# Two chunk loops with the 64x64 inverse issued as ten single products, one other block between each two

## The reference, cut to what matters

```python
def gdn_core(q, k, v, g, beta, s0):
    ...
    kb = k * beta[..., None]
    a_kk = jnp.einsum('bnhid,bnhjd->bnhij', kb, k) * jnp.exp(jnp.where(strict, seg, -jnp.inf))
    rhs = jnp.concatenate([kb * jnp.exp(gcum)[..., None], v * beta[..., None]], axis=-1)
    sol = lax.linalg.triangular_solve(a_kk, rhs, left_side=True, lower=True, unit_diagonal=True)
    ...
    a_qk = jnp.einsum('bnhid,bnhjd->bnhij', q, k) * jnp.exp(jnp.where(incl, seg, -jnp.inf))
    ...
    def step(s, xs):
        w_n, u_n, aqk_n, q_n, k_n, gl_n = xs
        v_new = u_n - w_n @ s
        o_n = q_n @ s + aqk_n @ v_new
        s = s * gl_n[..., None, None] + jnp.swapaxes(k_n, -1, -2) @ v_new
        return s, o_n

def rwkv_core(r, w, k, v, z, b, s0):
    def step(s, xs):
        r_t, w_t, k_t, v_t, z_t, b_t = xs
        sz = jnp.einsum('bhvk,bhk->bhv', s, z_t)
        s = (s * w_t[:, :, None, :] + sz[..., None] * b_t[:, :, None, :]
             + v_t[..., None] * k_t[:, :, None, :])
        return s, jnp.einsum('bhvk,bhk->bhv', s, r_t)
```

## Time and profile before

| | us |
|---|---|
| median of 3 runs | 2844.28 (2839.02 to 2854.64) |
| profiled execution | 2840.01 |
| its span, first to last instruction | 2838.3 |
| TensorE busy | 2509.7 (88%) |
| VectorE busy | 1565.3 (55%) |
| GpSimd busy | 837.4 (30%) |
| DeltaNet's chunk loop | 730.8 to 988.65 |
| the wide loop | 1165.7 to 1438.7 |

### The profile page before, as it was taken

The page is one execution under the profiler, slowest core; times in us unless marked ns, Lnnn a source line. Parts: engine busy times, 40 slices in busy tenths (PEclk is TensorE's granted clock), DMA queues, the critical chain, the costliest instruction groups (busy, mean ns, idle before and its releaser), DMA issues. The chain is left out here.

```text
span 2838.3 us, 72517 instructions
## 1 busy us (share of the span) xinstructions
PE 2509.7 (88%) x27195; PEld 1379.0 (49%) x27196; DVE 1565.3 (55%) x2859; ACT 968.9 (34%) x1707; POOL 837.4 (30%) x654
## 2 busy tenths in 40 slices
PE   5999899799677679789969897899999999999956
PEld 2448358445577645588844352333333333333322
DVE  3106276735367722556544486566666666666638
ACT  2603116312212112322211112455555555555511
POOL 1000000000343100111100002666666666666555
PEclk9999999899899989999979998999999999999978
DMA  6001302210000020000032207899998889772277
GB/s 254 2 0 46 137 15 90 87 36 1 2 3 4 3 72 1 2 4 4 4 113 89 101 1 294 303 344 350 366 354 315 336 323 352 271 296 89 74 298 317
DMA packets 109101, 408.12 MB, mean 144 GB/s; under 512 B 21002, under 2 KB 37084, under 8 KB 83933
## 3 DMA queue, kind: packets, MB, share of 16 engines
q1 hardware_dynamic: 76636, 287.71, 27.5%
q0 software_dynamic: 20736, 75.51, 6.8%
q10 hardware_dynamic: 11520, 41.95, 3.7%
HBM read 346.40 MB, written 58.72 MB: 143 GB/s over the span
## 5 line engine op out<-in xcount | busy, mean ns | idle before, releaser
L3198 PE MATMUL bank<-arena 128*32 x1280 | 567.4, 596 | 10.8 <-SPq L68 6.9
L3200 PE MATMUL bank<-arena 128*32 128x512 f32 x3840 | 568.4, 596 | 0.0
L3159 POOL COPY arena<-arena 128x2048 f32 x240 | 450.2, 1909 | 329.5 <-PE bank L3232 311.6
L3198 PEld LDWEIGHTS bank<-arena 128*32 128x32 f32 x1280 | 134.7, 110 | 358.6 <-issue 349.7
L3229 PE MATMUL bank<-arena 128*32 x640 | 289.3, 595 | 5.5 <-POOL arena L3159 5.5
L3232 PE MATMUL bank<-arena 128*32 128x512 f32 x1920 | 290.4, 595 | 0.0
L3353 DVE COPY arena<-arena 128x2048 f32 x80 | 138.5, 1731 | 203.8 <-PE bank L3200 185.8
L3290 ACT COPY arena<-arena 128x2048 f32 x80 | 152.0, 1900 | 204.4 <-PE bank L3200 142.9
L1255 PE MATMUL bank<-arena 64*64 64x64 f32 x4480 | 164.9, 224 | 58.3 <-DVE arena L1325 27.4
L3149 POOL DMA_INDIRECT arena<-normed_rows,arena x80 | 165.0, 2063 | 149.4 <-DVE arena L3337 137.4
L1255 PEld LDWEIGHTS bank<-arena 64*64 64x64 f32 x4480 | 149.1, 138 | 68.5 <-ACT arena L1315 22.0
(11 more groups left out here) (555 smaller groups left out, 4555.8 us busy)
## 6 DMA issues: line engine op xcount, KB each, us to landing
arena<-in_exp_w_gate_dram SPq DMA_DIRECT2D x64, 1024.0 KB
arena<-in_exp_w_up_dram SPq DMA_DIRECT2D x64, 1024.0 KB
arena<-in_exp_w_down_dram SPq DMA_DIRECT2D x64, 1024.0 KB
expert_rows<-arena ACTq DMA_DIRECT2D x80, 512.0 KB
arena<-in_w_mod_dram SPq DMA_DIRECT2D x32, 512.0 KB, 8.4
arena<-in_x_dram SPq DMA_DIRECT2D x16, 512.0 KB, 8.3
arena<-in_w_mod_dram SPq DMA_DIRECT2D x8, 1024.0 KB, 17.8
arena<-in_w_in_dram SPq DMA_DIRECT2D x12, 384.0 KB
```

The lines of the kernel that those rows point to most:

```text
L3159: last = nc.gpsimd.tensor_copy(down_copy(u), down_of(slots[u]))
L3198: nc.tensor.matmul(out(SUB - 1), XTT[:, b.q, c, rows(SUB - 1)], W[:, :, c], start=first, stop=end)
L3200: last = nc.tensor.matmul(out(u), XTT[:, b.q, c, rows(u)], WC[:, u, :, c], start=first, stop=end)
```

## The change: ten separate products, and grams, operands and turns split to lie between them

`weave` takes a table of stages with shifts (0: this pair, 1: the one ahead, -1: behind, 2: two ahead) and serves both loops; `weave_wide` is gone. The inverse's products are named, each is a stage of its own, and `fourth` and `eighth` stand apart from `y2` and `y4`. In DeltaNet the key gram is split into `rows` and `grams`, the query gram into `query rows` and `query grams`, and VectorE's part of the scan into `against` and `decay`. In the wide loop the four grams, the two operand groups (keys, queries) and the two turned operands (k, b) are stages of their own with semaphores of their own. The turn of the next pair's N0 moves from the head of its iteration to before t64 or y64 of the one before. No arithmetic is added or taken away; GpSimd's list in DeltaNet has its two stages under new names.

```diff
-    def tensor(self, pe, k, p):
+    def tensor(self, pe, what, p):
         N0, N32, N64, Y = (b[:, p % 2] for b in (self.N0, self.N32, self.N64, self.Y))
-        if k == 1:
-            self.dve_done(pe, p, "turned")
+        if what == "square":
+            pe.wait_ge(self.turned, p + 1)
             for n in range(2):
                 self.squared(n, self.M, N0)
-        elif k == 2:
+        elif what == "y2":
             self.act_done(pe, p, "square1")
-            self.dve_done(pe, p, "y1")
+            pe.wait_ge(self.begun, p + 1)
+            if p >= 1:
+                self.dve_done(pe, p - 1, "y64")
             self.product(2, self.N, Y)
+        elif what == "fourth":
             for n in range(2):
                 self.dve_done(pe, p, f"square{n}_turned")
                 self.squared(n, self.M, self.N)
-        elif k == 3:
+        elif what == "y4":
             self.act_done(pe, p, "fourth1")
             self.dve_done(pe, p, "y2")
             self.product(2, self.N, Y)
+        elif what == "eighth":
             for n in range(2):
                 self.dve_done(pe, p, f"fourth{n}_turned")
                 self.squared(n, self.M, self.N)
-        elif k == 4:
...
+        if what == "turn":
+            turn(self.M, self.N0[:, p % 2]).then_inc(self.turned, 1)
+            dve.wait_ge(self.turned, p + 1)
+            self.nc.vector.tensor_tensor(Y, self.M, each(self.c.ident, 8), ALU.add).then_inc(self.begun, 1)
+        elif what in ("square", "fourth"):
+            if what == "square":
+                dve.wait_ge(self.begun, p + 1)
             for n in range(2):
-                self.act_done(dve, p, f"square{n}")
-                turn(self.M[:, 4 * n:4 * n + 4], self.N[:, 4 * n:4 * n + 4])
-        elif k == 2:
-            add("y2", "y1")
-            for n in range(2):
-                self.act_done(dve, p, f"fourth{n}")
-                turn(self.M[:, 4 * n:4 * n + 4], self.N[:, 4 * n:4 * n + 4])
-        elif k == 3:
-            add("y4", "y2")
-        elif k == 4:
-            add("y8", "y4")
-        elif k == 5:
+                self.act_done(dve, p, f"{what}{n}")
+                turn(self.M[:, 4 * n:4 * n + 4], self.N[:, 4 * n:4 * n + 4]).then_inc(self.dve_s, 1)
+        elif what == "y2":
+            add("y2")
+        elif what == "y4":
+            self.dve_done(dve, p, "y2")
+            add("y4")
+        elif what == "y8":
+            self.dve_done(dve, p, "y4")
+            add("y8")
+        elif what == "t32":
             self.dve_done(dve, p, "y8")
-            turn(self.X, Y)
-        elif k == 6:
-            add("y32", "y8")
+            turn(self.X, Y).then_inc(self.dve_s, 1)
+        elif what == "y32":
+            add("y32")
             self.dve_done(dve, p, "y32")
-            turn(self.X, Y)
-        elif k == 8:
-            add("y64", "y32")
+            turn(self.X, Y).then_inc(self.dve_s, 1)
+        elif what == "y64":
+            add("y64")
 
...
+            def key_grams(p):
                 if p >= 1:
...
+            def query_rows(p):
+                if p < FIRST:
+                    return
+                pe.wait_ge(arg2, p + 1)
...
-            weave(PAIRS, none, gram_k, gram_q, none, none, none)
+            weave(PAIRS, DELTA_ORDER, None, {"grams": gram_k, "query grams": gram_q})
...
 
             def gram_k(p):
+                if p - 1 >= FIRST:
+                    dve.wait_ge(aq_rdy, p - FIRST)
                 dve.wait_ge(rows2, p + 1)
                 dve.wait_ge(mc2, p + 1)
                 TT(E, x8(b_row[:, :]), MC, ALU.add).then_inc(arg2, 1)
+
+            def key_grams(p):
                 if p >= 1:
                     dve.wait_ge(n_off, p)
+                dve.wait_ge(grams2, p + 1)
                 dve.wait_ge(exp2, p + 1)
                 STT(NF, x8(b_gram[:, :]), -1.0, E, ALU.mult, ALU.mult).then_inc(n_rdy, 1)
 
                 dve.wait_ge(mc3, p - FIRST + 1)
                 dve.wait_ge(n_rdy, p + 1)
                 TT(E, x8(b_row[:, :]), MC3, ALU.add).then_inc(arg3, 1)
+
+            def query_grams(p):
+                if p < FIRST:
+                    return
+                dve.wait_ge(grams3, p - FIRST + 1)
                 dve.wait_ge(exp3, p - FIRST + 1)
                 TT(AQ[:, p % 3], x8(b_gram[:, :]), E, ALU.mult).then_inc(aq_rdy, 1)
...
+            def decay(p, u):
...
-def weave(pairs, inv, gram_k, gram_q, against_state, solve, result):
-
-
-
-    for p in range(-1, pairs + 1):
-        now, ahead, behind = 0 <= p < pairs, p + 1 < pairs, p >= 1
-        for stage in range(9):
-            if now:
-                inv(stage, p)
-            if stage == 0 and ahead:
-                gram_k(p + 1)
-            if stage == 4 and ahead:
-                gram_q(p + 1)
-            if behind and stage in (1, 5):
-                against_state(p - 1, stage // 5)
-            if behind and stage in (2, 6):
-                solve(p - 1, stage // 5)
-            if behind and stage in (3, 7):
-                result(p - 1, stage // 5)
+def weave(pairs, order, inverse, stages):
+
+
+
+    for p in range(-2, pairs + 1):
+        for what, shift in order:
+            if not 0 <= p + shift < pairs:
+                continue
+            if what in stages:
+                stages[what](p + shift)
+            elif what in POWERS and inverse is not None:
+                inverse(what, p + shift)
+
+
+POWERS = ("turn", "square", "y2", "fourth", "y4", "eighth", "y8", "t32", "y32", "t64", "y64")
+DELTA_ORDER = (("square", 0), ("against 0", -1), ("y2", 0), ("solve 0", -1), ("decay 0", -1), ("fourth", 0),
+               ("rows", 1), ("result 0", -1), ("y4", 0), ("grams", 1), ("eighth", 0), ("query rows", 1), ("y8", 0),
+               ("against 1", -1), ("t32", 0), ("solve 1", -1), ("decay 1", -1), ("y32", 0), ("result 1", -1), ("turn", 1),
+               ("t64", 0), ("query grams", 1), ("y64", 0))
+WIDE_ORDER = (("square", 0), ("prepare keys", 1), ("right 0", -1), ("y2", 0), ("prepare queries", 1), ("solve 0", -1),
+              ("fourth", 0), ("gram zb", 1), ("y4", 0), ("result 0", -1), ("gram zk", 1), ("eighth", 0), ("gram rb", 1),
+              ("y8", 0), ("gram rk", 1), ("t32", 0), ("right 1", -1), ("y32", 0), ("solve 1", -1), ("turn k", 1),
+              ("t64", 0), ("result 1", -1), ("turn b", 1), ("turn", 1), ("exps", 2), ("y64", 0))
 
...
+            def gram_zb(p):
+                pe.wait_ge(keys, p + 1)
                 if p >= 1:
                     pe.wait_ge(tb, p)
-                gram(b_a, ZS[:, p % 3], BS)
-                gram(b_b, KS, ZS[:, p % 3]).then_inc(n_ps, 1)
-
-            def gram_q(p):
-                if p < FIRST:
-                    return
-                pe.wait_ge(azk, p + 1)
-                gram(b_a, BS, RS[:, p % 3])
-                gram(b_b, KS, RS[:, p % 3]).then_inc(q_ps, 1)
-
-            def gram_t(p):
+                gram(b_a, ZS[:, p % 3], BS).then_inc(zb_ps, 1)
+
+            def gram_zk(p):
+                pe.wait_ge(queries, p + 1)
+                if p >= 1:
+                    pe.wait_ge(tk, p)
+                gram(b_b, KS, ZS[:, p % 3]).then_inc(zk_ps, 1)
+
+            def gram_rb(p):
+                if p >= FIRST:
+                    pe.wait_ge(n_rdy, p + 1)
+                    gram(b_a, BS, RS[:, p % 3]).then_inc(rb_ps, 1)
+
+            def gram_rk(p):
+                if p >= FIRST:
+                    pe.wait_ge(azk, p + 1)
+                    gram(b_b, KS, RS[:, p % 3]).then_inc(rk_ps, 1)
...
-            def prepare(p):
+            def prepare_keys(p):
                 dve.wait_ge(expd, p + 1)
                 if p >= 1:
-                    dve.wait_ge(t_ps, p)
+                    dve.wait_ge(tb_ps, p)
...
+            def gram_zb(p):
+                dve.wait_ge(zb_ps, p + 1)
                 if p >= 1:
                     dve.wait_ge(n_off, p)
                 masked(NF, b_a, H.strict).then_inc(n_rdy, 1)
+
+            def gram_zk(p):
+                dve.wait_ge(zk_ps, p + 1)
                 masked(AZK[:, p % 3], b_b, strictT).then_inc(azk, 1)
 
-            def gram_q(p):
-                if p < FIRST:
-                    return
-                dve.wait_ge(q_ps, p - FIRST + 1)
-                masked(ABR[:, p % 3], b_a, H.causal)
-                masked(AKR[:, p % 3], b_b, H.causal).then_inc(abr, 1)
+            def gram_rb(p):
+                if p >= FIRST:
+                    dve.wait_ge(rb_ps, p - FIRST + 1)
+                    masked(ABR[:, p % 3], b_a, H.causal).then_inc(abr, 1)
+
...
```

More of the change, by code:

```diff
@@ L1779, in result @@
                 last.then_inc(outs, 1)
-            weave(PAIRS, lambda stage, p: inv.tensor(pe, stage, p), gram_k, gram_q, against_state, solve, result)
+            weave(PAIRS, DELTA_ORDER, lambda what, p: inv.tensor(pe, what, p),
+                  {"rows": rows, "grams": key_grams, "query rows": query_rows, "query grams": query_grams,
```

(29 more changed lines are left out.)

184 lines of the change are left out of this document (99 added, 85 removed).

## The result

The changed kernel takes 2804.82 us (median of four executions, 2802.77 to 2809.69); the kernel before, measured with it, 2846.77. The ratio is 0.9851, 95% interval 0.9827 to 0.9876: 42 us faster. The profiled execution took 2804.22 us, span 2802.5. Lines of the changed kernel are numbered differently: turn L1324 (before L1320), additions to Y L1328, beginning of Y L1334, products L1256, squares L1264.

What follows compares the result with a forecast made beforehand. No engine is full; TensorE waits on latencies of a chain in both loops. DeltaNet -11 and wide loop -32 give -43 us against the profiled 2840.0, so 2797; the median lies 4.3 higher: 2801 us, forecast 2785 to 2810.

Runs made afterwards that it cites:

- the last order above: Kernel with early mask terms and early wide turn, plus each DeltaNet solve set one product further from its right side: 2771.2 us, ratio 0.9726.

## What to carry to other kernels

When an order is rewritten for the engine that is the bound, walk the other engines' queues through it too: here a sum came to stand ahead of its data from GpSimd, and everything queued behind it on VectorE, critical or not, waited along. The producer's order has to be moved with the consumer's; those four instructions of GpSimd, moved for nothing, were worth 33 us after the change and nothing before it. And a stall is to be priced with the clock that it brings down behind it (here 4 us and 1.1). And a loop is to be compared with more than one profile of before: with the same order of stages DeltaNet's took 258 to 263 us here.

## What the runs showed of the hardware

- Filling eight stalls of 4 us with four products each whose results nobody reads made the kernel 8 us faster: the granted clock around the stall stayed at 1.00 where it had been 0.66 in the 5 us behind it (2.4 GHz is the upper of its two levels, 1.2 the lower).
- Two 128x128 subtractions on VectorE with both inputs in SBUF took 0.49 us together beside an idle GpSimd, 0.89 beside its instructions of 0.4 us (eight pairs of the changed kernel), and 1.67 to 2.49 beside those of 1.3 us (and the last order above). The same two instructions cost up to five times as much by where they stand.
